# A chain of layer norms in a two-block transformer: the second norm's mean and variance from weighted moments of the first norm's centred input

## The chip, the cores and the metric

The kernel runs on one core of one Trainium2 chip. The time is the device time of one launch in microseconds (us). A core has five engines that run side by side, each through its own instruction list in order: TensorE (PE, matmuls and their weight loads), VectorE (DVE), ScalarE (ACT), GpSimd (POOL) and SyncE (SP, which here only issues DMAs). They meet through semaphores: an instruction can wait until another engine has done something, and everything queued behind it on its own engine waits too.

## What is computed

The model is a hybrid block (width 1024, 528 tokens) followed by a second block of two layers on 512 latent and 256 context tokens. All the work of this change is in the second block. Cut to the norms, one of its layers is:

```
def layer_norm(x):
    mu = jnp.mean(xf, -1, keepdims=True)
    var = jnp.mean(jnp.square(xf - mu), -1, keepdims=True)
    return (xf - mu) * lax.rsqrt(var + LN_EPS)
def modulate(x, shift, scale):
    return layer_norm(x) * (1 + scale) + shift
for l in range(2):
    h = modulate(x, sh1, sc1)                               # norm a
    y = mixing_sublayer(h, ...)
    x = layer_norm(ALPHA * x + g1 * y) * ln1_g + ln1_b      # norm b
    h = modulate(x, sh2, sc2)                               # norm c
    x = layer_norm(ALPHA * x + g2 * swiglu(h)) * ln2_g + ln2_b   # norm d
```

The output of b is the input of c, and also the residual for d. The output of d in layer 0 is the input of a in layer 1. So three times in the program a layer norm with a learned gain and bias feeds a second layer norm directly: b0 to c0, d0 to a1, b1 to c1.

## The kernel before

Everything is fp32. Activations lie transposed: the 1024 features are 8 tiles of 128 partitions, the tokens are columns, in chunks of 256: in layer 0 of the second block three chunks (the context, numbered 0, and two of latent tokens), in layer 1 two. An fp32 product is three matmuls (lines 1053 to 1055) on a high and a low half of weights and activations. SP fetches weight tiles of 128x1024, ACT makes the high half (line 1582) and DVE the low half (line 2155).

A layer norm is a chain of steps over all engines, since the sum over features is a sum over partitions, which only TensorE does cheaply:

- **mean**: eight matmuls of 128x32 ones against the eight feature tiles, four of them side by side in the four quarters of the array (`quarter_sums`, line 1235). ACT copies the four partial sums out of PSUM (`evacuate`, line 1682), and one more 128x128 matmul adds them up and spreads the result over the partitions (`total`, line 1255; step **centre**).
- DVE subtracts the mean, in two halves of 128x1024 (line 2276), and ACT squares both halves (line 1694).
- **square** and **root**: the same eight matmuls, copy and single matmul on the squares give the variance.
- ACT makes a first guess of 1/sqrt by a logarithm and an exponential (lines 1707 and 1709, `guess`), DVE corrects it with one Newton step of three 128x256 instructions (lines 2264 to 2268) after one that adds epsilon (line 2283).
- **apply**: DVE multiplies both halves by the root (line 2297), ACT applies gain and bias, one feature tile at a time (line 1730, eight instructions). A norm that feeds a matmul also needs the high and low half of its result, called X2: ACT writes the high half (line 1735), DVE the low half of the first four tiles (line 2301), POOL that of the last four (line 2855, `lows`).

ACT holds one set of function tables at a time. The logarithm and exponential need one set (loaded at line 1700), the silu of the FFN (line 1743) another, and changing is an instruction of its own on ACT.

The order of the work is planned when the program is built. `chain` (line 621) turns a list of norms and a chunk number into steps, each with the PE time it is thought to take and with the time after which the next step may follow. `woven` (line 653) runs through a list of matmul items and puts a step of a chain between two items as soon as it is due. All engines then run the same list of steps, each with its own part of a step. In a layer (`latent_sequence`, line 757) the items around a b-to-c chain are the eight output projections `oo` of each chunk; the chain of a chunk begins 2.0 after its last projection. Behind them come the FFN items `fa` and `fb`: they are taken chunk by chunk, a chunk's first only when its chain has ended, and no chunk may be more than five items ahead of the slowest. So the last chunk's chain has little to run under: once the other chunks have had their five items, TensorE waits for the last chunk's X2. The same holds at the end of layer 0, where chain d0, a1 stands before the projections of layer 1. `latent_sequence` plans chains of `[b, c_]` and of `[d, a]`, that is eight steps with two normalisations one after the other.

## Time and profile before

| | |
|---|---|
| median of 3 runs | 3517.22 us (3512.65 to 3518.37) |
| profiled execution | 3517.82 us, span of its trace 3516.0 us |
| mean granted TensorE clock | 0.967 of full speed |
| busy share | PE 93%, PEld 86%, DVE 47%, ACT 39%, POOL 13% |
| HBM | 301.57 MB read, 86 GB/s over the span |

PE is matmuls, PEld the weight loads that overlap them. Times in rows are microseconds from the start of the span. A span is the time from the first to the last instruction in the trace; the time of the execution is 1.8 us more.

The context chunk and two latent chunks of layer 0 go through b0, c0 at about 2000 to 2125, through d0, a1 at about 2640 to 2750; the two latent chunks of layer 1 go through b1, c1 at about 3045 to 3130.

### The profile page before, as it was taken

The numbers are of one execution on the slowest core, as the hardware profiler recorded it, in microseconds if no ns is written. First come the engines' busy times: TensorE is split into PE (matmuls) and PEld (weight loads), VectorE is DVE, ScalarE is ACT, GpSimd is POOL, SyncE is SP. The second block draws the span as 40 slices with busy tenths as digits, with TensorE's granted clock in tenths as the row PEclk, the third lists the DMA queues.
The fourth block names the chain that finished last, engine by engine and source line by source line (L and its number), as shares of the span: only waits on it lengthen the run. The fifth ranks groups of instructions, "written<-read, shape, count | busy, mean of one in ns | idle before, by whom it ended". The sixth has DMA issues, their size and how long they took to land. (4 is left out here: it accounts for less than half of the span.)

```text
span 3516.0 us, 59585 instructions
## 1 busy us (share of the span) xinstructions
PE 3263.2 (93%) x24536; PEld 3033.4 (86%) x24552; DVE 1661.9 (47%) x2754; ACT 1358.7 (39%) x2387; POOL 468.0 (13%) x466
## 2 busy tenths in 40 slices
PE   6999999999899899998989878999997899879998
PEld 5999987877688899997889868999995789769997
DVE  3666643447634456664346642222236436633234
ACT  3222322247623322234358553122235447542223
POOL 1010110135400010010014001000000014010100
PEclk9999999999999999999999989999998899989999
DMA  4444321111022244541102311111122202312222
GB/s 139 168 160 171 139 84 62 60 55 43 19 96 96 91 150 167 177 149 58 55 10 75 114 55 61 61 59 62 61 88 74 69 29 63 125 50 95 85 94 93
DMA packets 90379, 313.03 MB, mean 89 GB/s; under 512 B 10048, under 2 KB 14400, under 8 KB 89984
## 3 DMA queue, kind: packets, MB, share of 16 engines
q1 hardware_dynamic: 86736, 296.06, 25.2%
q0 software_dynamic: 2944, 12.63, 1.1%
q8 instruction: 198, 3.24, 0.4%
q14 instruction: 69, 0.57, 0.1%
q10 hardware_dynamic: 432, 0.52, 0.0%
HBM read 301.57 MB, written 2.10 MB: 86 GB/s over the span
## 5 line engine op out<-in xcount | busy, mean ns | idle before, releaser
L2155 DVE TENSOR_TENSOR r_Wbasel<-r_Wf,r_Wbaseh 128x1024 fp32r<-128x1024 f32 (+1 forms) x292 | 366.4, 1256 | 555.0 <-ACT r_Wbaseh L1582 554.7
L1582 ACT ACTIVATE r_Wbaseh<-r_Wf 128x1024 fp32r<-128x1024 f32 (+1 forms) x292 | 301.2, 1036 | 463.1 <-PE PS L1055 355.4
L1053 PE MATMUL PS<-r_X2h,r_Wbaseh 128*128 128x256 f32 (+1 forms) x1336 | 416.2, 311 | 51.0 <-DVE r_X2l L2301 37.3
L1053 PE MATMUL PS<-r_X1h,r_Wbaseh 128*128 128x264 f32 (+2 forms) x1216 | 393.3, 323 | 17.2 <-DVE r_Wbasel L2155 10.7
L1055 PE MATMUL PS<-r_X2h,r_Wbasel 128*128 128x256 f32 (+1 forms) x1336 | 406.1, 304 | 0.0
L1054 PE MATMUL PS<-r_X2l,r_Wbaseh 128*128 128x256 f32 (+1 forms) x1336 | 404.2, 303 | 0.0
L1054 PE MATMUL PS<-r_X1l,r_Wbaseh 128*128 128x264 f32 (+2 forms) x1216 | 380.2, 313 | 0.0
L1055 PE MATMUL PS<-r_X1h,r_Wbasel 128*128 128x264 f32 (+2 forms) x1216 | 379.6, 312 | 0.0
L2155 DVE TENSOR_TENSOR r_Wtopl<-r_Wf,r_Wtoph 128x1024 fp32r<-128x1024 f32 (+1 forms) x165 | 197.3, 1197 | 293.0 <-ACT r_Wtoph L1582 292.4
L1053 PEld LDWEIGHTS PS<-r_X2h,r_Wbaseh 128*128 128x128 f32 x1336 | 260.7, 195 | 69.2 <-ACT r_XC L1730 23.8
L1054 PEld LDWEIGHTS PS<-r_X2l,r_Wbaseh 128*128 128x128 f32 x1336 | 263.3, 197 | 11.1 <-issue 2.6
L1053 PE MATMUL PS<-r_X2h,r_Wtoph 128*128 128x256 f32 x872 | 251.2, 288 | 20.0 <-DVE r_X2l L2301 17.5
L1055 PEld LDWEIGHTS PS<-r_X2h,r_Wbasel 128*128 128x128 f32 x1336 | 260.2, 195 | 7.9
L1053 PEld LDWEIGHTS PS<-r_X1h,r_Wbaseh 128*128 128x128 f32 x1216 | 232.2, 191 | 39.6 <-DVE r_Wbasel L2155 14.2
L1054 PE MATMUL PS<-r_X2l,r_Wtoph 128*128 128x256 f32 x872 | 250.0, 287 | 0.0
L1055 PE MATMUL PS<-r_X2h,r_Wtopl 128*128 128x256 f32 x872 | 249.8, 287 | 0.0
L1054 PEld LDWEIGHTS PS<-r_X1l,r_Wbaseh 128*128 128x128 f32 x1216 | 232.5, 191 | 15.1 <-issue 2.4
L1055 PEld LDWEIGHTS PS<-r_X1h,r_Wbasel 128*128 128x128 f32 x1216 | 232.3, 191 | 13.1
L1582 ACT ACTIVATE r_Wtoph<-r_Wf 128x1024 fp32r<-128x1024 f32 (+1 forms) x165 | 168.5, 1025 | 161.0 <-PE PS L1055 86.6
L1743 ACT ACTIVATE r_TM<-PS 128x256 f32<-128x256 f32 (+1 forms) x198 | 76.3, 386 | 367.0 <-PE PS L1055 366.8
L1053 PE MATMUL PS<-r_X1h,r_Wtoph 128*128 128x264 f32 (+1 forms) x672 | 191.3, 285 | 7.8 <-DVE r_Wtopl L2155 7.8
L1054 PE MATMUL PS<-r_X1l,r_Wtoph 128*128 128x264 f32 (+1 forms) x672 | 190.9, 284 | 0.0
(369 smaller groups left out, 8727.2 us busy)
## 6 DMA issues: line engine op xcount, KB each, us to landing
r_Wf<-in_wmod SPq DMA_DIRECT2D x96, 512.0 KB, 3.5
r_Wf<-in_f_in SPq DMA_DIRECT2D x88, 512.0 KB, 4.3
r_Wf<-in_g_in SPq DMA_DIRECT2D x88, 512.0 KB, 3.4
r_Wf<-in_g_out SPq DMA_DIRECT2D x56, 448.0 KB, 3.3
r_Wf<-in_w_o SPq DMA_DIRECT2D x40, 512.0 KB, 4.4
r_Wf<-in_f_out SPq DMA_DIRECT2D x32, 448.0 KB, 4.2
r_Wf<-in_f_out SPq DMA_DIRECT2D x16, 512.0 KB, 4.4
r_Wf<-in_g_out SPq DMA_DIRECT2D x16, 512.0 KB, 3.4
```

Of the source, the lines that this page charges most:

```text
L1053: self.e.matmul(o, wh, xh, start=first, stop=False)
L1054: self.e.matmul(o, wh, xl, start=False, stop=False)
L1055: return self.e.matmul(o, wl, xh, start=False, stop=last)
L1582: e.activation(p.w(i, cols)[0], p.Wf[:, i % NW, 0:cols], ACT.Copy).then_inc(*p.hi.did(i))
L1743: e.activation(f.tm(c), p.psb(p.bank(("fa", f.tag, j, c)), f.chunks[c][1]), ACT.Silu).then_inc(*p.act.did(("silu", f.tag, j, c)))
L2155: e.tensor_tensor(l, p.Wf[:, i % NW, 0:cols], h.bitcast(F32), ALU.subtract).then_inc(*p.lo.did(i))
```

## The change

With z the centred input of the first norm, r its reciprocal root, g and b its gain and bias and b' = b - mean(b), the output is y = r g z + b. Hence

mean(y) = r mean(g z) + mean(b), and var(y) = r (r (mean(g² z²) - mean(g z)²) + 2 mean(g b' z)) + mean(b'²).

So the second norm M's statistics come from four sums over z and z² of the first norm N: z² with weights 1 and g², z with weights g and g b'. The weights are a matrix WM of 128 x 32 columns per feature tile, 16 columns each; a matrix MS picks one or the other half when the quarters are added up. `N.pair(M)` marks such a pair (b0 with c0, b1 with c1, d0 with a1). Norms d1, n1 to n3 and a0 are as before. In a pair:

- TensorE has one mean, one centre, then 16 quarter matmuls (`squares`: four each on z and z², twice) and four single matmuls (`root_sums`).
- ACT copies three partial sums instead of four, squares two halves instead of four and squares mean(g z) once (128x256).
- DVE gets five instructions of 128x256 for the second variance, and `second_applied`: it rebuilds M's centred input from y (a scalar_tensor_tensor of 128x1024), multiplies by the second root, and makes the low half. The second guess and Newton step follow without any matmul.
- Step `second` carries the second root and N's gain and bias on ACT, step `both` (once for each half) M's normalisation; ACT in `both` has half a norm: four identities and the high copy.
- POOL fetches MS (128x256) and WM (128x512 per norm) behind the attention of each layer; two steps `moments` per norm make mean(b), b', mean(b'²) and the weights (two matmuls of 8 columns and a few small DVE instructions).
- The planner has other numbers: seven steps for the pair.

```
@@ -622,6 +653,11 @@
     for N in norms:
+        if N.then is not None:
+            out += [(("mean", N, i), 1.0, 0.9), (("centre", N, i), 0.5, 4.0), (("square", N, i), 1.8, 1.5),
+                    (("root", N, i), 1.7, 7.0), (("second", N, i), 0.0, 5.0), (("both", N, i, 0), 0.0, 5.0),
+                    (("both", N, i, 1), 0.0, 7.0)]
+            continue
         if not N.rms:
...
-    chains = [(chain([b, c_], c), ("oo", l, 7, c), 2.0) for c in range(nc)]
+    chains = [(chain([b], c), ("oo", l, 7, c), 2.0) for c in range(nc)]
...
-        chains += [(chain([d, a], c), ends[c], 2.0) for c in range(nc)]
+        chains += [(chain([d], c), ends[c], 2.0) for c in range(nc)]
...
@@ -1257,6 +1305,53 @@
+    def squares(self, N, i):
...
+        for g in (0, 1):
+            e.wait_ge(*p.dve.of(("xs", N.id, i, g)))
+            x = self.quarter_sums(c, lambda k: N.xc(i, 4 * g + k), g, n, lambda k: N.weights(k, 1))
+            if g == 1:
+                x.then_inc(*p.mm.did(("cross", N.id, i)))
+            e.wait_ge(*p.act.of(("sq", N.id, i, g)))
+            x = self.quarter_sums(b, lambda k: N.sq4(i, g)[:, k, :], g, n, lambda k: N.weights(k, 0))
+        x.then_inc(*p.mm.did(("square", N.id, i)))
+
+    def root_sums(self, N, i):
...
+        e.matmul(p.psb(b, n), one, ss, start=True, stop=True).then_inc(*p.mm.did(("var", N.id, i)))
...
+        e.matmul(p.psb2(b, 0, n), one, sc, start=True, stop=True)
+        e.matmul(p.psb2(b, 256, 256 + n), two, ss, start=True, stop=True).then_inc(
+            *p.mm.did(("gz", N.id, i), ("squares", N.id, i)))
...
+        e.matmul(p.psb(b, n), two, sc, start=True, stop=True).then_inc(
+            *p.mm.did(("gbz", N.id, i), ("crosses", N.id, i)))
@@ -1623,6 +1718,15 @@
...
+        elif what == "square" and a[0].then is not None:
+            N, i = a
+            self.evacuate(N, "crosses", "cross", i, 1.0 / 1024)
+            self.evacuate(N, "squares", "square", i, 1.0 / 1024)
+        elif what == "second":
+            self.second_root(*a)
+            self.first_applied(*a)
+        elif what == "both":
+            self.second_applied(*a)
@@ -1715,6 +1822,36 @@
...
+    def second_root(self, N, i):
+
+        self.e.wait_ge(*self.p.dve.of(("var2", N.id, i)))
+        self.guess_of(N.row(i, 3), N.row(i, 2), N.bvar, ("guess2", N.id, i))
+
+    def first_applied(self, N, i):
+        p, e = self.p, self.e
+        for g in (0, 1):
+            e.wait_ge(*p.dve.of(("xn", N.id, i, g)))
...
+    def second_applied(self, N, i, g):
...
+        e.wait_ge(*p.dve.of(("xn", M.id, i, g)))
...
+        e.wait_ge(*p.act.of(("end", M.id, i, 4 * g + 3)))
+        e.activation(M.to4(i, g, 0), M.xc4(i, g), ACT.Copy).then_inc(*p.act.did(("high", M.id, i, g)))
@@ -2284,6 +2430,80 @@
...
+    def first_root(self, N, i):
...
+        self.newton(x, r, t, p.act.of(("guess", N.id, i)), 1.0, ("rsqrt", N.id, i))
...
+        e.tensor_tensor(u, ggzz, u, ALU.subtract).then_inc(*dve.did(k("gvar")))
+        e.wait_ge(*dve.of(k("gvar")))
+        e.tensor_tensor(u, u, r, ALU.mult).then_inc(*dve.did(k("gvar_r")))
+        e.wait_ge(*p.mm.of(k("gbz")))
+        e.wait_ge(*dve.of(k("gvar_r")))
+        e.scalar_tensor_tensor(u, p.psb(p.bank(k("gbz")), n), 2.0, u, ALU.mult, ALU.add).then_inc(
+            *dve.did(k("twice")))
+        e.wait_ge(*dve.of(k("twice")))
+        e.tensor_tensor(v, u, r, ALU.mult).then_inc(*dve.did(k("var2")))
+        e.tensor_tensor(gzr, gz, r, ALU.mult).then_inc(*dve.did(k("gzr")))
+        self.scaled_by_root(N, i, 0, r)
...
+    def second_root(self, N, i):
...
+        e.tensor_scalar(x, v, N.bvar, None, ALU.add).then_inc(*dve.did(("eps2", N.id, i)))
+        self.scaled_by_root(N, i, 1, r)
+        e.wait_ge(*dve.of(("eps2", N.id, i)))
+        self.newton(x, y, t, p.act.of(("guess2", N.id, i)), 1.0, ("rsqrt2", N.id, i))
+
+    def second_applied(self, N, i, g):
...
+        e.wait_ge(*p.act.of(("end", N.id, i, 4 * g + 3)))
+        e.scalar_tensor_tensor(M.xc4(i, g), N.h4(i, g), N.bmean, N.wide(N.row(i, 1), i), ALU.subtract,
+                               ALU.subtract).then_inc(*dve.did(("xs", M.id, i, g)))
+        e.wait_ge(*dve.of(("xs", M.id, i, g)))
+        e.tensor_tensor(M.xc4(i, g), M.xc4(i, g), N.wide(N.row(i, 3), i), ALU.mult).then_inc(
+            *dve.did(("xn", M.id, i, g)))
```

How the lists move, first on TensorE, in layer 1, where the last chunk's b stands together with chunk 0's second norm. Names are the program's: r_H holds b's input and, in place, its centred and normalised form, r_SQ the squares, r_PA the partial sums, r_CF the ones, r_WM and r_MS the new weights, r_X2h and r_X2l the input of the FFN. Before:

```order
L1235 MATMUL PS<-r_H,r_CF 32x256 x16
L1255 MATMUL PS<-r_PA,r_CF 128x256 x2
L1235 MATMUL PS<-r_SQ_114,r_CF 32x256 x16
L1255 MATMUL PS<-r_PA,r_CF 128x256 x2
L1053 MATMUL PS<-r_X2h,r_Wtoph 128x256
L1054 MATMUL PS<-r_X2l,r_Wtoph 128x256
```

After:

```order
L1284 MATMUL PS<-r_H,r_CF 32x256 x8
L1303 MATMUL PS<-r_PA,r_CF 128x256
L1284 MATMUL PS<-r_H,r_WM 32x256 x4
L1284 MATMUL PS<-r_SQ_114,r_WM 32x256 x4
L1284 MATMUL PS<-r_H,r_WM 32x256 x4
L1284 MATMUL PS<-r_SQ_114,r_WM 32x256 x4
L1346 MATMUL PS<-r_PA,r_MS 128x256
L1349 MATMUL PS<-r_PA,r_MS 128x256
L1350 MATMUL PS<-r_PA,r_MS 128x256
L1353 MATMUL PS<-r_PA,r_MS 128x256
L1093 MATMUL PS<-r_X2h,r_Wtoph 128x256
L1094 MATMUL PS<-r_X2l,r_Wtoph 128x256
```

Chunk 0's second mean and variance, which shared the place with the last chunk's first ones, are gone. Further on, before, the last chunk's own second mean and variance stood among the FFN matmuls (eight of line 1235 and one of line 1255, each twice); after, none does.

On ACT, same place, from the high halves of weights through the end of chunk 0's b. Here r_Wtoph and r_Wbaseh are high halves of weights, r_H is b's result (line 1730, 1840 after), r_XC_121 is c's (1851 after). Before:

```order
L1707 ACTIVATE r_RS<-PS,r_V 128x256
L1709 ACTIVATE r_RS<-r_RS 128x256
L1730 ACTIVATE r_H<-r_H,r_V 128x256 x8
L1582 ACTIVATE r_Wtoph<-r_Wf 128x1024
L1582 ACTIVATE r_Wbaseh<-r_Wf 128x1024 x2
L1682 ACTIVATE r_PA<-PS 128x256 x2
L1694 ACTIVATE r_SQ_114<-r_XC_121 128x4x256 x2
L1694 ACTIVATE r_SQ_114<-r_H 128x4x256 x2
```

After:

```order
L1677 ACTIVATE r_Wtoph<-r_Wf 128x1024
L1677 ACTIVATE r_Wbaseh<-r_Wf 128x1024 x2
L1814 ACTIVATE r_SQ_114<-r_SQ_114,r_MB 128x256
L1816 ACTIVATE r_SQ_114<-r_SQ_114 128x256
L1840 ACTIVATE r_H<-r_H,r_V 128x256 x8
L1786 ACTIVATE r_PA<-PS 128x256
L1798 ACTIVATE r_SQ_114<-r_H 128x4x256 x2
L1851 ACTIVATE r_XC_121<-r_XC_121,r_MOD 128x256 x4
```

The three copies of weights moved ahead of the eight instructions that apply b's gain, and the second guess (1814, 1816) stands ahead of those eight. The last chunk's partial sum (1786) now comes behind them. On DVE the new small instructions stand between the first root and the first wide multiplication, and weight splits and residual additions between the two wide ones:

```order
L2468 TENSOR_TENSOR r_SQ_114<-PS,r_SQ_114 128x256
L2470 TENSOR_TENSOR r_SQ_114<-r_SQ_114,r_RS 128x256
L2473 SCALAR_TENSOR_TENSOR r_SQ_114<-PS,r_SQ_114 128x256
L2476 TENSOR_TENSOR r_SQ_114<-r_SQ_114,r_RS 128x256
L2477 TENSOR_TENSOR r_SQ_114<-PS,r_RS 128x256
L2482 TENSOR_TENSOR r_H<-r_H,r_RS 128x4x256
L2292 TENSOR_TENSOR r_Wtopl<-r_Wf,r_Wtoph 128x1024
L2553 SCALAR_TENSOR_TENSOR r_H<-PS,r_MOD,r_H 128x256
L2292 TENSOR_TENSOR r_Wbasel<-r_Wf,r_Wbaseh 128x1024
```

What was one piece of two multiplications (line 2297 before) is now two, with other work between them: three weight splits (2292) and three residual additions (2553) in all.

## Rows read from the trace of the kernel before

**Rows 1.** The page, busy time, share of the span and instructions of each engine
```profile
PE 3263.2 (93%) x24536; PEld 3033.4 (86%) x24552; DVE 1661.9 (47%) x2754; ACT 1358.7 (39%) x2387; POOL 468.0 (13%) x466
```

**Rows 2.** Waits of TensorE: line, releaser, us in total, times, longest
```profile
PE PS L1053 <- DVE r_X2l L2301: 54.8, 7, 9.6
```

**Rows 3.** Stretches: length, busy us (and count) of PE PEld DVE ACT POOL, PEclk, DMA
```profile
2150.00:2600.00 450.00, 450.00 (x3753) 450.00 (x3752) 108.62 (x157) 95.10 (x164) 39.91 (x54) 1.00 0.19 61
2057.85:2123.49 65.64, 41.65 (x305) 35.98 (x305) 24.35 (x31) 39.09 (x61) 7.63 (x6) 0.81 0.08 28
2695.61:2748.22 52.61, 29.16 (x160) 20.09 (x161) 22.96 (x26) 28.78 (x48) 4.71 (x2) 0.63 0.03 10
3068.88:3126.91 58.03, 33.63 (x209) 25.24 (x209) 26.20 (x30) 34.58 (x55) 6.18 (x4) 0.68 0.08 29
```

**Rows 4.** Timeline, b1 and c1 of the last chunk: start, us, engine, instruction, [idle before]
```profile
3039.38 1.07 PE L1235 MATMUL PS<-r_H,r_CF 128*32 128x256 f32 x16
...
3068.88 0.38 ACT L1682 ACTIVATE r_PA<-PS 128x256 f32<-128x256 f32 x1 [3.83 <-PE PS L1235]
3070.02 2.35 DVE L2276 TENSOR_TENSOR r_XC<-r_H,PS 128x1024 f32<-128x1024 f32 x2 [2.42 <-PE PS L1255]
...
3092.66 4.04 ACT L1730 ACTIVATE r_H<-r_H,r_V 128x256 f32<-128x256 f32 x8 [4.12 <-DVE r_H L2297]
3097.67 1.28 ACT L1743 ACT_TABLE_LOAD   x1
3099.24 0.38 ACT L1682 ACTIVATE r_PA<-PS 128x256 f32<-128x256 f32 x1
3102.32 0.59 PE L1255 MATMUL PS<-r_PA,r_CF 128*128 128x256 f32 x2
3102.95 2.35 DVE L2276 TENSOR_TENSOR r_XC<-r_H,PS 128x1024 f32<-128x1024 f32 x2
...
3113.19 1.28 ACT L1700 ACT_TABLE_LOAD   x1
3114.48 0.47 ACT L1707 ACTIVATE r_RS<-PS,r_V 128x256 f32<-128x256 f32 x1
3116.88 2.36 DVE L2297 TENSOR_TENSOR r_XC<-r_XC,r_RS 128x1024 f32<-128x1024 f32 x2
3118.20 2.08 ACT L1730 ACTIVATE r_XC<-r_XC,r_MOD 128x256 f32<-128x256 f32 x4 [2.80 <-DVE r_XC L2297]
3120.31 1.06 ACT L1735 ACTIVATE r_X2h<-r_XC 128x1024 fp32r<-128x1024 f32 x1
3121.40 1.22 DVE L2301 TENSOR_TENSOR r_X2l<-r_XC,r_X2h 128x1024 fp32r<-128x1024 f32 x1 [2.16 <-ACT r_X2h L1735]
3122.77 0.55 PE L1053 MATMUL PS<-r_X2h,r_Wtoph 128*128 128x256 f32 x1 [9.61 <-DVE r_X2l L2301]
3124.50 2.35 POOL L2855 TENSOR_TENSOR r_X2l<-r_XC,r_X2h 128x1024 fp32r<-128x1024 f32 x1 [14.05 <-ACT r_X2h L1735]
3126.91 0.58 PE L1053 MATMUL PS<-r_X2h,r_Wtoph 128*128 128x256 f32 x1 [1.24 <-POOL r_X2l L2855]
```

**Rows 5.** Groups by line and shape, 2625 to 3130: count, busy us, mean ns, idle before
```profile
L1694 ACT ACTIVATE r_SQ<-r_H 128x1024 f32<-128x1024 f32 x10 | 10.6, 1060 | 9.7 <-DVE r_H L2276 9.2
L1682 ACT ACTIVATE r_PA<-PS 128x256 f32<-128x256 f32 x20 | 7.6, 378 | 25.3 <-PE PS L1235 25.2
L2268 DVE SCALAR_TENSOR_TENSOR r_RS<-r_RS 128x256 f32<-128x256 f32 x11 | 4.7, 425 | 0.4
```

**Rows 6.** Groups by line and shape, the whole trace
```profile
L2241 DVE SCALAR_TENSOR_TENSOR r_JK<-r_Wf,r_CR 128x1024 f32<-128x1024 f32 x96 | 117.0, 1218 | 0.0
L1235 PE MATMUL PS<-r_SQ,r_CF 128*32 128x256 f32 x368 | 30.3, 439 | 7.9 <-ACT r_SQ L1694 4.2 <-DVE r_XC L2276 3.3
```

More of the change, by code:

```diff
@@ L667, in woven @@
             out.append(s)
-            if s[0] == "root":
+            if s[0] == "root" and s[1].then is None:
                 out.append(("apply", *s[1:]))
@@ L1167, in step @@
         elif what == "square":
-            self.square(*a)
+            if a[0].then is None:
+                self.square(*a)
+            else:
+                self.squares(*a)
         elif what == "root":
-            self.root_sum(*a)
+            if a[0].then is None:
+                self.root_sum(*a)
+            else:
+                self.root_sums(*a)
+        elif what == "moments":
+            self.moments(*a)
         elif what == "mod":
@@ L2195, in step @@
         elif what == "root":
-            self.root_norm(*a)
+            if a[0].then is None:
+                self.root_norm(*a)
+            else:
+                self.first_root(*a)
+        elif what == "second":
+            self.second_root(*a)
+        elif what == "both":
+            self.second_applied(*a)
+        elif what == "moments":
+            self.moments(*a)
         elif what == "apply":
@@ L2286, in root_norm, with moments @@
         self.newton(x, y, t, p.act.of(("guess", N.id, i)), 1.0, ("rsqrt", N.id, i))
+    def moments(self, N, last):
+        p, e, dve = self.p, self.e, self.p.dve
+        key = ("bvar" if last else "bmean", N.id)
+        e.wait_ge(*p.mm.of(key))
+        e.tensor_reduce(N.bvar if last else N.bmean, p.psb(p.bank(key), 8), AX, ALU.add).then_inc(*dve.did(key))
+        e.wait_ge(*dve.of(key))
+        if not last:
+            e.tensor_scalar(N.b1, p.vec8(N), N.bmean, None, ALU.subtract).then_inc(*dve.did(("b1", N.id)))
+            e.wait_ge(*dve.of(("b1", N.id)))
+            e.tensor_tensor(N.b2, N.b1, N.b1, ALU.mult).then_inc(*dve.did(("bsquare", N.id)))
+            return
+        e.tensor_scalar(N.bvar, N.bvar, N.then.eps, None, ALU.add).then_inc(*dve.did(("bvar2", N.id)))
+        e.wait_ge(*p.load(("moments", N.id)).of("in"))
+        w = N.WM[:, :, 16:32]
+        e.tensor_tensor(w, w, w, ALU.mult).then_inc(*dve.did(("gg", N.id)))
+        w = N.WM[:, :, 48:64]
+        e.tensor_tensor(w, w, N.b1.unsqueeze(2).broadcast_to([128, 8, 16]), ALU.mult).then_inc(
+            *dve.did(("weights", N.id)))
@@ L2827, in step @@
             self.lows(*a)
+        elif what == "both":
+            N, i, g = a
+            if g == 1:
+                self.lows(N.then, i)
         elif what == "bar":
@@ L3241, in _layout @@
     a["vec"] = v
+    g = np.stack([cols(i[f"ln{n}_g_2"][l]) for n, l in ((1, 0), (2, 0), (1, 1))])
+    g = np.broadcast_to(g[:, :, :, None, None], (3, 128, 8, 2, 32)).copy()
+    g[:, :, :, 0, 0:16] = 1.0
+    a["wmom"] = g
     return a
```

120 lines of the change are left out of this document (110 added, 10 removed).

## The prediction

> **What bounds the kernel now.** I read the page's busy times first. TensorE is busy 3263.2 of 3516.0 us, 93% [rows 1], so a gain must come out of the 253 us in which it idles, or out of stretches where it runs at a lowered clock. Then the waits of TensorE: the largest group by far is the first matmul on X2, 54.8 us in seven waits, the longest 9.6 [rows 2]. X2 is what the second norm of a pair hands to the FFN or to the next projections. Then the stretches: from 2150 to 2600, in the middle of an FFN, TensorE is busy 450.00 of 450.00 us at full clock, while DVE and ACT have 109 and 95. In the three stretches from the last chunk's first mean to the second half of its X2 it is busy 41.65 of 65.64, 29.16 of 52.61 and 33.63 of 58.03 us, at a granted clock of 0.81, 0.63 and 0.68 of full [rows 3], between its two levels. They hold 24.0, 23.5 and 24.4 us of idle time, 72 in all, and no other engine is full either. The bound there is the chain of small steps of the last chunk. Since TensorE is full behind each of them, what is saved there reaches the end of the program.
>
> The timeline shows that chain for b1, c1 of the last chunk [rows 4]. The mean's partial sums are copied at 3068.88; b is done at 3096.70 (3092.66 + 4.04); c then needs a table load and silu of the FFN that stand before its copy on ACT, its copy at 3099.24, its single sum at 3102.32, centring at 3102.95, squares and their sums, a table load at 3113.19, the guess at 3114.48, multiplication 3116.88, gain 3118.20, high half 3120.31, low half 3121.40, TensorE at 3122.77; the second half waits for POOL until 3126.91. From b's end to c's guess there are 17.8 us (3114.48 - 3096.70). This is the piece that the change rewrites.
>
> **The change part by part.** *Removed from the path, per pair:* c's mean, copy, sum, centring, two squares, eight sums, copy and sum, that is those 17.8 us.
>
> *Put in its place.* After N's root DVE has five more small instructions: 425 ns each [rows 5]. Between the logarithm's end (3114.48 + 0.47) and the multiplication at 3116.88 [rows 4] lie four of this kind in a chain, so one costs 0.46 to 0.48 with its hop, and five 2.3 us. ACT squares mean(g z), 0.4 us by the 378 of a copy of the same shape [rows 5]. The second guess then only needs the second variance, and runs on ACT ahead of N's gain; its Newton step lies beside the eight gain instructions (4.04 us [rows 4]). Behind these DVE rebuilds M's centred input with a wide scalar_tensor_tensor: 1218 ns for 128x1024 in another place of the program [rows 6], the same as the subtraction (2.35 for two [rows 4]), and multiplies it, 1.2. So from N's gain to M's gain stand 2.4 us on DVE in place of about 18 to 20.
>
> *TensorE's own work.* Sixteen quarter matmuls took 1.07 us at full clock [rows 4], 439 ns each as single records, which overlap [rows 6]. Before a pair had 32 quarter matmuls and four single ones, now it has 24 (8 + 16) and five (1 + 4): at 1.07 per 16 and 0.3 each that is 2.14 + 1.2 = 3.3 before, 1.6 + 1.5 = 3.1 after. Nothing of note; at half clock twice that.
>
> *ACT* loses two squares of 1.06 and one copy of 0.38 [rows 5] and gains 0.42; *DVE* has 2.3 us more in small and as many wide instructions as before (nine). Over eight pairs ACT has 17 us less, DVE 18 more, at 47% busy; only what of it is on the chain counts.
>
> *The moments and the new DMAs.* POOL fetches MS and WM when the attention is done, ahead of all output projections (no row shows such a load); POOL is at 13% [rows 1], TensorE gets two matmuls of 8 columns per norm. I cost them at nothing, covered by the output projections; if the cover fails, each of three places waits a few us for a load, 10 us at most in all, which is inside the range.
>
> *The order.* On ACT the last chunk's first copy now stands behind the eight gain instructions of chunk 0, and these wait for DVE's second wide multiplication, which stands behind three weight splits and three residual additions. So it comes later: 3069.7 by my walk, against 3068.88. I walked every engine's list of the changed program through this stretch, giving each instruction the later of its operands and its engine, with the durations of these rows:
> - copy of the mean 3069.7 (+0.8); centring 3070.9 to 3073.25; meanwhile DVE rebuilds M of chunk 0 until 3075.65, and ACT has its gain and high half until 3078.9, then copies the two partial sums of the last chunk (3079.7).
> - four single sums at half clock, 3082.9; ACT, busy with the second half of chunk 0, comes to the first guess at 3083.3 to 3083.8 and the small square at 3084.3.
> - Newton 3085.3, five small ones 3087.6, first wide multiplication 3088.8; then ACT has a weight split, a gated FFN tile with its high half and a table load before the second guess, 3094.5.
> - gain of N 3098.5 (eight, 4.04); another table load and a silu, 3100.2; M's rebuild and multiplication 3103.1 behind a gating on DVE; four gains and high half 3106.3; low half, TensorE 3107.7 (before 3122.77 [rows 4]); the second half through POOL 3112.3 (before 3126.91).
>
> That is 14.6 us. Of the 17.8 removed and 2.4 put in, 15.4 would be left if nothing else moved; 2.3 for small instructions and 1 for the late start count against it, and the new order gives some of it back. The same walk gives, for layer 0's b0, c0, X2 of the last chunk at 2105.1 in its second half against the end of the first stretch, 2123.49 [rows 3]: 18.4. For d0, a1 it gives 2731.7 against 2748.22 [rows 3]: 16.5. The sum is 49.5. The stretches have 24.0, 24.4 and 23.5 us of idle time, so no term asks for more than there is, and the same matmuls (33.63 us of 43.4 left for b1) still fit. The walk has ideal hops between engines in some places, 0.1 to 0.2 us each; I take 1.5 off for them: 48.
>
> Sum against the profiled execution: 3517.8 - 48 = 3469.8. It stands 0.6 above the median, which is less than I can tell: 3470.
>
> *A rule that speaks against.* The trace has a table load of 1.28 us at 3113.19 and the guess at 3114.48 [rows 4], 0.01 after its end, so no drain is seen behind a load. The path of the last chunk has two table loads more than before in b0, c0 and one more in b1, c1, since guess and silu now alternate; that is in the walk. The Trainium skill, "ScalarE: Activation LUTs", section "What ACT_TABLE_LOAD costs", gives 1283 ns for the load and about 1380 ns for a drain with each. By that page three more loads would cost an estimated 4 us more and the time be about 3474; the row shows the load alone, and I go by it.
>
> **Bounds of what the trace does not show.** The quarter matmuls with different weights in the four quarters: the nearest rows are 1.07 for sixteen with equal weights, and 439 ns each if they did not lie side by side. At the upper end, 16 x 0.44 = 7.0 in place of 1.07 x (1 to 2), some 5 more per pair and up to 40 for eight pairs if none of it is hidden. I take the lower end, since the weight loads are instructions of the same kind. Wide scalar_tensor_tensor with a row broadcast over four tiles and a per-partition scalar: 1.22 for the subtraction with the same broadcast, 1.22 for the row of this operation; a second operand in SBUF instead of PSUM may do either way, at most 0.3 each, 2 us in all. The new loads 0 to 10. The walk's placing of FFN items in ACT's and DVE's lists: each misplaced item delays a step by 1 to 1.7 (a split of 128x1024 as the square 1.06 [rows 5], table load and a copy-sized silu 1.28 + 0.38 [rows 4, 5]); two or three per place give minus 12 to plus 10 in all.
>
> **Rivals.**
> - *Half the gain.* ACT takes its list in order, and between root and second guess stand splits, gatings, silus that wait for TensorE, which itself waits. If at each place another round of these (table load, silu, load back, about 4, twice) falls on the path, the gain is 8 less each: 24 in all, 3494. For: TensorE's wait for the last X2 was 9.6 us with one such round on the path [rows 2, 4]. Against: the walk already has each of these items.
> - *Quarter sums not side by side.* 40 less of 49.5: gain 10, 3508. For: weights now differ for each quarter and each tile, so each needs its own load. Against: before, every quarter matmul has its own load record too, and they ran at 1.07 per 16.
> - *The waits only move.* The last chunk's X2 stays where it was, because something else (weights, partial sums of the FFN in order) ends there: 3517. Against: the seven waits name DVE's X2l [rows 2], and nothing else ends there.
> - *Slower.* One mechanism: the late first guess. The second root and N's gain are now one step and stand behind FFN items; if the chunk ahead of the last also comes later, TensorE runs out earlier, its clock falls, and the sums at half clock (3.1 x 2) and copies are all on the path. Price: copy 3.3 later (three copies of weights), sums 2.4 more, per place 5.7 with nothing saved by the shorter second chain: 17 over three places, 3535. It decides if the last chunk's X2 begins more than 54 us after its first copy (3122.77 - 3068.88 = 53.9 [rows 4]).
>
> **How the numbers follow.** A measurement of this kernel tells apart about 0.2%, 7 us. Forecast 0.68, its own range 3457 to 3484 (the placing and the loads). Half the gain 0.17 at 3494. Sums not side by side 0.03 at 3508. Waits only move 0.05 at 3517. Slower 0.07 at 3535. The range 3450 to 3503 holds the first two, about 0.85 less the edges. Faster by more than 7 us: 0.68 + 0.17 + 0.03 = 0.88; same 0.05; slower 0.07.
>
> **What the profile after would show.** The wait of TensorE for r_X2l falls from 54.8 to below 30 us. In the three places from the last chunk's first copy to its second half of X2: about 43 us for b1 (58.0 before), 46 for b0 (65.6), 36 for d0 (52.6). Sixteen quarter sums with WM in about 1.1 us at full clock. The last chunk's second guess about 11 us after its first. Busy times: ACT down 17, DVE up about 18, PE the same. I am wrong if the stretches shorten and the time does not, if X2's first half still begins 50 us or more after the copy, or if the copy itself comes over 3 us later than TensorE's last output projection would have it.

## The result

The changed kernel takes 3465.95 us (median of 4 runs, 3461.35 to 3469.64), the kernel before on the same occasion 3517.80. The ratio is 0.9854, 95% interval 0.9837 to 0.9871: a gain of 51.9 us, 1.5%. The forecast was 3470 with its own range 3457 to 3484. Later, beside the experiments, the same kernel gave 0.9862 (0.9849 to 0.9876), 3469.8 us.

The span of the profiled execution is 3459.5 us, 56.5 less than before. Its busy times, page part 1:

```profile
PE 3237.1 (94%) x24436; PEld 3021.6 (87%) x24452; DVE 1679.3 (49%) x2815; ACT 1338.9 (39%) x2369; POOL 479.2 (14%) x471
```

Against [rows 1] ACT has 19.8 us less and DVE 17.4 more, close to the 17 and 18 of the forecast. TensorE has 26 us less at 100 records less, where the forecast had "the same". An estimated 9 us of it are the fewer and shorter sums (below); for the rest I can only argue that less of its work falls in stretches of lowered clock, since the mean granted clock rose from 0.967 to 0.972.

The waits of TensorE (line, releaser, us, times, longest):

```profile
PE PS L1093 <- DVE r_X2l L2505: 26.4, 3, 10.3
PE PS L1303 <- ACT r_PA L1786: 14.0, 8, 4.7
PE PS L1316 <- DVE r_MB L2444: 7.8, 1, 7.8
PE PS L1093 <- DVE r_X2l L2521: 5.5, 1, 5.5
```

The first row and the last together answer to [rows 2], since a norm outside the pairs now makes its low half at a line of its own: 31.9 us in four waits where there were 54.8 in seven. That is a little above the forecast's "below 30". Six of the seven lay at the three places, two at each, 49.3 us; now there is one at each, for the last chunk, 26.4 us. The second row is TensorE waiting for the copy of a mean's partial sums. The third is new: it is a moment step of d0, planned between two output projections. TensorE stood 7.8 us in it, because the instruction it waits for is behind the first root of another chunk on DVE.

The three stretches that answer to those of [rows 3], from the last chunk's first copy of partial sums to the second half of its X2, and the same part of b1's timeline as in [rows 4]:

```profile
2054.80:2102.40 47.60, 33.26 (x254) 30.77 (x253) 25.47 (x32) 30.83 (x53) 9.40 (x6) 0.86 0.07 23
2672.68:2708.07 35.39, 20.23 (x127) 15.69 (x127) 23.50 (x27) 22.84 (x42) 4.74 (x2) 0.76 0.00 1
3026.80:3070.37 43.57, 26.23 (x174) 21.71 (x174) 26.86 (x31) 28.85 (x49) 7.46 (x4) 0.71 0.08 26
```

```profile
3026.80 0.36 ACT L1786 ACTIVATE r_PA<-PS 128x256 f32<-128x256 f32 x1
...
3039.84 0.46 ACT L1814 ACTIVATE r_RS<-PS,r_V 128x256 f32<-128x256 f32 x1
...
3041.99 1.28 ACT L1880 ACT_TABLE_LOAD   x1
...
3049.62 0.42 ACT L1890 ACTIVATE r_H3h<-r_TM 128x256 fp32r<-128x256 f32 x1 [4.08 <-DVE r_TM L2529]
...
3050.05 1.28 ACT L1804 ACT_TABLE_LOAD   x1
...
3051.35 0.51 ACT L1814 ACTIVATE r_SQ<-r_SQ,r_MB 128x256 f32<-128x256 f32 x1
...
3056.26 1.28 ACT L1880 ACT_TABLE_LOAD   x1
3057.56 0.38 ACT L1880 ACTIVATE r_TM<-PS 128x256 f32<-128x256 f32 x1
3058.03 0.42 DVE L2529 TENSOR_TENSOR r_TM<-r_TM,PS 128x256 f32<-128x256 f32 x1 [4.28 <-ACT r_TM L1880]
3058.37 1.28 DVE L2498 SCALAR_TENSOR_TENSOR r_XC<-r_H,r_MB,r_SQ 128x1024 f32<-128x1024 f32 x1
...
3061.41 2.08 ACT L1851 ACTIVATE r_XC<-r_XC,r_MOD 128x256 f32<-128x256 f32 x4 [2.50 <-DVE r_XC L2501]
...
3065.97 0.55 PE L1093 MATMUL PS<-r_X2h,r_Wtoph 128*128 128x256 f32 x1 [10.30 <-DVE r_X2l L2505]
...
3070.37 0.58 PE L1093 MATMUL PS<-r_X2h,r_Wtoph 128*128 128x256 f32 x1 [1.50 <-POOL r_X2l L3088]
```

After the pair's four single sums, the last of which ends at 3040.75, no sum over features stands on the chain any more. The second guess is 11.5 us later (forecast about 11). X2's first half comes 39.2 us after the first copy; before it was 53.9. The stretches are 47.6, 35.4 and 43.6 us; the forecast said 46, 36 and 43.

Single profiles differ by several us outside the three places: the changed kernel's profile and its repeat are 3.4 us apart at the start of b0 and 8.7 at the end of b1, while the places themselves agree to 0.4 us. So from here on I compare the three *places* by their length: each from a copy of chunk 0's partial sums (in b0 that of its squares, in a pair the first of the two copies; in d0 and b1 that of its mean) to TensorE's first matmul on the second half of the last chunk's X2. Each number is the difference of two starts in a timeline.

| kernel | b0 | d0 | b1 | sum | ratio to before (95%) | median us |
|---|---|---|---|---|---|---|
| before | 124.66 | 119.16 | 86.40 | 330.2 | | 3517.8 |
| changed | 107.66 | 100.68 | 71.95 | 280.3 | 0.9854 (0.9837 to 0.9871) | 3465.95 |
| changed, repeat | 107.69 | 100.68 | 72.27 | 280.6 | 0.9862 (0.9849 to 0.9876) | 3469.8 |
| b, c pairs only | 107.11 | 119.15 | 71.78 | 298.0 | 0.9910 (0.9894 to 0.9927) | 3482.6 |
| d, a pair only | 127.49 | 100.68 | 86.80 | 315.0 | 0.9952 (0.9937 to 0.9967) | 3497.8 |
| before, earlier steps | 124.01 | 122.71 | 87.02 | 333.7 | 1.0002 (0.9993 to 1.0012) | 3517.6 |
| ten more on DVE | 119.91 | 113.53 | 81.35 | 314.8 | 0.9950 (0.9935 to 0.9964) | 3497.5 |
| moments early | 107.13 | 100.67 | 71.86 | 279.7 | 0.9844 (0.9829 to 0.9859) | 3459.75 |
| second at 1.0 | 109.50 | 106.49 | 75.80 | 291.8 | 0.9900 (0.9884 to 0.9917) | 3480.95 |
| second and both at 1.0 | 111.68 | 105.08 | 70.3 | 287.1 | 0.9889 (0.9874 to 0.9904) | 3476.8 |
| split gain | 103.12 | 97.34 | 68.16 | 268.6 | 0.9833 (0.9817 to 0.9848) | 3458.2 |
| combined | 102.02 | 97.37 | 68.16 | 267.6 | 0.9823 (0.9809 to 0.9836) | 3454.3 |
| combined, lows on POOL | 105.74 | 98.8 | 68.47 | 273.0 | 0.9833 (0.9819 to 0.9847) | 3460.8 |
| combined, no silu | 101.02 | 96.17 | 65.35 | 262.5 | 0.9793 (0.9779 to 0.9806) | 3444.35 |

The three places give 17.0 + 18.5 + 14.5 = 49.9 us of the gain, measured from the unrounded sums. The stretch from 3126.91 to the end of the span before and from 3070.37 after is 389.1 us in both.

### The profile page after: what moved, and what is told of

The parts are those of the page before. It is cut to its first block and busy times, and to the rows that moved or that the text cites. A ratio compares the mean times of both kernels' runs of the same rounds, so it can differ in the third digit from the quotient of the medians.

```text
span 3459.5 us, 59413 instructions
## 1 busy us (share of the span) xinstructions
PE 3237.1 (94%) x24436; PEld 3021.6 (87%) x24452; DVE 1679.3 (49%) x2815; ACT 1338.9 (39%) x2369; POOL 479.2 (14%) x471
## 5 line engine op out<-in xcount | busy, mean ns | idle before, releaser
L1093 PE MATMUL PS<-r_X1h,r_Wbaseh 128*128 128x264 f32 (+2 forms) x1216 | 391.2, 322 | 17.6 <-DVE r_Wbasel L2292 11.4
L1093 PE MATMUL PS<-r_X2h,r_Wtoph 128*128 128x256 f32 x872 | 249.4, 286 | 11.8 <-DVE r_X2l L2505 10.3
L3045 POOL TENSOR_TENSOR r_H3l<-r_TM,r_H3h 128x256 fp32r<-128x256 f32 x110 | 84.5, 768 | 793.1 <-ACT r_H3h L1890 793.1
```

Source lines behind the costliest of these rows:

```text
L1093: self.e.matmul(o, wh, xh, start=first, stop=False)
L3045: e.tensor_tensor(hl, f.tm(c), hh.bitcast(F32), ALU.subtract).then_inc(*p.pool.did(("hid", f.tag, j, c)))
```

## The experiments

### One kind of pair alone

Edit for b, c only:

```
-        self.norms["d0"].pair(self.norms["a1"])
...
-        items[-2:-2] = [(("moments", d, False), 0, None)]
-        items.append((("moments", d, True), 0, None))
...
-        chains += [(chain([d], c), ends[c], 2.0) for c in range(nc)]
+        chains += [(chain([d, p.norms["a1"]], c), ends[c], 2.0) for c in range(nc)]
...
```

> Only b0 to c0 and b1 to c1 are pairs; d0 and a1 are as in the kernel before. My theory: the gain is made at three separate places, each by the last chunk's shorter chain, and adds up. The trace of the changed kernel puts 21.1 us at b0, 19.1 at d0 and 16.4 at b1. So this run has a span 37.5 us shorter than before (about 3478.5) and TensorE's place between d0 and a1 looks as before, 52.6 us. Rival: the gain is a matter of the new step numbers and orders over the whole layer, and the places are not independent; then this run is more than 6 us away from that.

Measured: 3482.6 us, ratio 0.9910; span 3474.9. The place at d0 is 119.15 us, before 119.16; b0 and b1 are those of the changed kernel within 0.6. The pairs' gains are independent: what the sum claimed. (The span is 41.1 us shorter than before, not 37.5, which is still within the 6 us; the places give 17.55 + 14.62 = 32.2, the rest of the span's difference lies outside them, 6.5 of it ahead of b0.)

For d, a only the edit is the mirror image (`b.pair(n)` and its moment steps out, `chain([b, c_], c)` back in, MS waited for in d0).

> Only d0 to a1 is a pair. By my theory (independent places) the span is 19 us shorter than before, about 3497; if the places are not independent it is more than 6 us away. A third possibility: without the other pair the two small moment steps of d0, which held TensorE 7.8 us in the changed kernel, cost another amount, since their neighbours change; then their wait shows it.

Measured: 3497.8 us, ratio 0.9952, span 3497.5. The place at d0 is 100.68 us, the same hundredth as in the changed kernel. b0 is 127.49, 2.8 us *longer* than before, though b0 and c0 work as before: the moment steps of d0 stand in it. TensorE waits there:

```profile
2052.73 0.57 PE L1313 MATMUL PS<-r_MB,r_CF 128*128 128x8 f32 x2 [13.10 <-DVE r_MB L2441]
```

Thirteen us of waiting stand beside 2.8 us in the place. In the kernel before TensorE also waited in this part of b0, at other instructions: 9.6 us in four waits, the longest 4.6. So there are only 3.5 us more of waiting, and that is near what the place lost. That the steps are the cause is read from the row; no run has this kernel with them elsewhere. The medians add up as the places do: 34.8 us for b, c alone and 19.7 for d, a alone, 54.5 together, against 51.9 for both.

### The order alone

```
-        out += [(("square", N, i), 1.0, 0.9), (("root", N, i), 0.5, 8.5 if N.dst is None else 7.5 if N.rms else 9.0)]
+        out += [(("square", N, i), 1.0, 0.9), (("root", N, i), 0.5, 5.0 if N.dst is None else 7.5 if N.rms else 9.0)]
```

> The kernel before, with one number of the planner changed: the norms b and d finish their apply step 5.0 instead of 8.5 after the root, as near as the steps of the changed kernel stand. If the gain is the arithmetic (a second mean and variance taken off the chain), this gives at most 3 us per place and at most 9 in all, more likely 0 to 4. If the gain is mostly the new order of steps among FFN items, it gives 20 us or more.

Measured: ratio 1.0002 (0.9993 to 1.0012), d0 even 3.5 us longer. Earlier steps without the new arithmetic give nothing. So the gain is what was taken off the chain, as far as one number of the planner can show it: the changed kernel's order differs in more than this number, and that order as a whole was not tried without the new arithmetic.

### Ten more small instructions

```
+        for j in range(10):
+            e.tensor_tensor(gzr, gz, r, ALU.mult).then_inc(*dve.did(k(f"again{j}")))
+            e.wait_ge(*dve.of(k(f"again{j}")))
         e.tensor_tensor(gzr, gz, r, ALU.mult).then_inc(*dve.did(k("gzr")))
```

> The changed kernel with ten more 128x256 instructions on DVE per pair, behind the second variance and ahead of the first wide multiplication (the same product made again). They take about 10 x 0.46 = 4.6 us. By my theory the last chunk's chain sets the end at all three places, so the span grows by 10 to 14 us, 4.6 at each less what stands hidden behind ACT's wait for the FFN items ahead of the second guess. Rival: at these places the chain waits for in-order FFN items (table loads, gatings) and not for DVE's arithmetic; then it grows by 5 or less.

Measured: 3497.5 us, 34.5 us more at the three places, and 35.1 in the span. Both theories fall, mine by a factor of about two and a half even at its upper end. The ten take 4.54 us:

```profile
3078.11 4.54 DVE L2478 TENSOR_TENSOR r_SQ<-PS,r_RS 128x256 f32<-128x256 f32 x10
```

The stretches of this kernel, first those from the copy of chunk 0 to the last chunk's first copy, then those from there on:

```profile
1995.46:2064.60 69.14, 52.04 (x421) 47.66 (x414) 54.44 (x90) 36.28 (x59) 2.41 (x1) 0.90 0.31 106
2620.88:2695.32 74.44, 55.43 (x455) 49.48 (x455) 56.22 (x88) 38.38 (x63) 2.41 (x1) 0.90 0.29 96
3026.26:3059.15 32.89, 26.09 (x226) 23.31 (x226) 25.14 (x41) 16.10 (x25) 0.00 (x0) 0.94 0.35 116
2064.60:2115.37 50.77, 33.67 (x259) 31.18 (x257) 29.62 (x42) 30.82 (x53) 9.39 (x6) 0.85 0.07 22
2695.32:2734.41 39.09, 20.81 (x127) 16.40 (x127) 27.65 (x37) 22.94 (x42) 4.72 (x2) 0.63 0.00 0
3059.15:3107.61 48.46, 26.00 (x174) 21.47 (x175) 31.09 (x41) 28.84 (x49) 7.45 (x4) 0.76 0.07 25
```

In the changed kernel the first three are these:

```profile
1994.74:2054.80 60.06, 51.59 (x424) 47.96 (x417) 46.05 (x70) 36.18 (x59) 2.40 (x1) 0.91 0.36 121
2607.39:2672.68 65.29, 55.31 (x455) 49.61 (x455) 47.74 (x68) 38.42 (x63) 2.41 (x1) 0.92 0.35 109
2998.42:3026.80 28.38, 25.66 (x226) 23.27 (x226) 20.96 (x31) 16.01 (x25) 0.00 (x0) 1.00 0.42 137
```

So the last chunk's own stretch grows by 3.2, 3.7 and 4.9, 11.8 in all, as my theory had it. But the part ahead of it grows by 9.1, 9.2 and 4.5: two earlier chunks in b0 and d0, one in b1, 4.5 to 4.6 us for each, every bit of the ten instructions. DVE works its list in order, and behind a chunk's small instructions stand the weight splits and residual additions of the next projections, on which the last chunk's mean depends. Per instruction it is 34.5 / 80 = 0.43 us. The change itself added five to each of eight pairs: if the rate holds for them too, which no run tests, they take back an estimated 17 us. I had costed them at 2.3 us per place, 7 in all, with only part of the rest in the walk.

### The moment steps earlier

```
+        if l == 0 and m in (3, 6):
+            items.append(("moments", d, m == 6))
...
-        items[-2:-2] = [(("moments", d, False), 0, None)]
-        items.append((("moments", d, True), 0, None))
+        pass
```

> The changed kernel with d0's two moment steps planned among chunk 0's output projections, behind b0's, in place of the end of the projections, where TensorE waited 7.8 us in them. My theory: that wait is in front of FFN work that is done ahead anyway, and counts only as far as it makes the last chunk's first mean late. The run with b, c pairs alone, which has no such step, was 3.6 us better at these places than the changed kernel's share (41.1 against 37.5). So the span falls by 3 to 4 us, to about 3456. If the wait is fully on the path it falls by 7 to 8, if it is hidden by less than 1.

Measured: the wait is gone, and the places are 0.6 us shorter, 0.5 of them in b0. In the combined kernel the same edit gives 1.1 in b0 (102.02 against 103.12 with the split alone). The median of 3459.75 lies 6.2 us below the changed kernel's, the span of the profile 3.1 above it; the intervals of the two ratios overlap, so the times say nothing more. My 3 to 4 came from a difference of spans (41.1 - 37.5) that was mostly offset outside the places. The places say under 1, as the third case had it. The trace shows why so little comes of it. With the moment steps gone, TensorE waits a few us later for the same DVE list, for the residual additions ahead of the last chunk's mean, and then for that mean's copy:

```profile
2054.02 1.08 PE L1285 MATMUL PS<-r_H,r_CF 128*32 128x256 f32 x8 [6.44 <-DVE r_H L2554]
2060.45 0.67 PE L1304 MATMUL PS<-r_PA,r_CF 128*128 128x256 f32 x2 [1.42 <-ACT r_PA L1787]
```

In the changed kernel neither of the two waited over 0.6 us. So the wait of 7.8 us did not end, it moved: DVE sets the time at which the last chunk can start, and TensorE idles for it at one instruction or at another.

### The second guess ahead of FFN items

```
-                    (("root", N, i), 1.7, 7.0), (("second", N, i), 0.0, 5.0), (("both", N, i, 0), 0.0, 5.0),
-                    (("both", N, i, 1), 0.0, 7.0)]
+                    (("root", N, i), 1.7, 1.0), (("second", N, i), 0.0, 5.0), (("both", N, i, 0), 0.0, 5.0),
+                    (("both", N, i, 1), 0.0, 13.0)]
```

> The changed kernel with the step second planned 1.0 instead of 7.0 behind the root, and the last step's number raised by the same 6, so that TensorE's own order is nearly the same, while on ACT and DVE the second guess stands ahead of some FFN items. The last chunk's second variance was ready at 3045.5 and its guess ran at 3051.35, behind a silu, a gated high half and a table load. If these in-order items hold the chain, the three places gain 3 to 6 us each and the span falls by 9 to 18. The rival is that ACT and DVE then wait in the step while TensorE needs weight splits queued behind it, for five pairs that are not the last chunk's: then it gains nothing or loses up to 10.

Measured: 3480.95 us, the places 11.5 us longer. The last chunk's own stretches are 43.3, 32.3 and 40.6 us, that is 4.3, 3.1 and 2.9 *shorter*: what stood in front of the second guess did hold the chain. The last chunk's second guess now comes 4.3 us after its first at all three places, in the changed kernel 9.3, 7.7 and 11.5. But the parts ahead of them grow more:

```profile
1999.91:2066.07 66.16, 55.12 (x430) 50.54 (x422) 48.43 (x72) 39.55 (x63) 2.35 (x1) 0.92 0.33 110
2612.81:2686.96 74.15, 56.69 (x455) 50.41 (x455) 50.40 (x70) 41.76 (x68) 2.35 (x1) 0.90 0.30 96
3013.77:3048.94 35.17, 26.09 (x226) 23.31 (x226) 23.41 (x33) 19.26 (x31) 0.00 (x0) 0.92 0.33 110
```

by 6.1, 8.9 and 6.8. Both theories are right, each in its part of the place; the rival is larger, and with 11.5 us at the places, 15.0 in the medians, larger than the 10 it was given. An edit of this kind for the last chunk alone was not tried.

> As the run before it, but the two steps both also planned at 1.0 each (the last number raised again). The whole second half of the pair then stands on ACT and DVE in one piece, with almost no FFN item inside. By the theory that in-order items hold the last chunk's chain this gains 2 to 3 us more per place for the table load and silu between N's gain and M's (3056.26 to 3057.94 in the changed kernel); by the rival (weight splits late for TensorE) it is slower than the run before it, by up to 15.

Its edit is 1.0 also for `second` and the first `both`, 21.0 for the last. Measured: 3476.8 us, places 287.1, 6.8 above the changed kernel and 4.7 below the run before it. In b1 it is 1.6 us better than the changed kernel, in b0 and d0 4.0 and 4.4 worse. Against the run before it b1 gains 5.5 and d0 1.4, and b0 loses 2.2, so neither the theory's 2 to 3 us per place nor the rival's loss came; the intervals of the two ratios overlap.

### The gain instructions split

```
             self.second_root(*a)
-            self.first_applied(*a)
+            self.first_applied(*a, 0)
         elif what == "both":
+            if a[2] == 0:
+                self.first_applied(*a[:2], 1)
             self.second_applied(*a)
...
```

> The changed kernel with the second four of N's eight gain instructions moved on ACT from the step second into the first step both, ahead of M's first four. M's first half needs only the first four, so DVE's rebuild and multiplication (2.5 us) then lie beside the second four (2.1 us), and the next chunk's first copy no longer waits for DVE's second wide multiplication. Expected 2 us less at each of the three places and about 1 for the earlier copy in b1, so the span falls by 5 to 8. If the gatings of the FFN hold DVE at that point anyway, it falls by less than 2.

Measured: 3458.2 us, ratio 0.9833; the places are 4.5, 3.3 and 3.8 us shorter, 11.7 in all, more than the 5 to 8 I said; the medians differ by 7.7, within them, with intervals of the ratios that overlap. Of these only 2.3, -0.4 and 1.2 lie in the last chunk's own stretch, 3.1 together. The larger part is ahead: the last chunk's first copy comes 2.2, 3.8 and 2.6 us sooner after chunk 0's. In b1 of the changed kernel it stood behind chunk 0's second four gain instructions, which waited 3.71 us for DVE:

```profile
3023.57 1.22 DVE L2482 TENSOR_TENSOR r_H<-r_H,r_RS 128x1024 f32<-128x1024 f32 x1
...
3024.82 2.07 ACT L1840 ACTIVATE r_H<-r_H,r_V 128x256 f32<-128x256 f32 x4 [3.71 <-DVE r_H L2482]
...
3026.80 0.36 ACT L1786 ACTIVATE r_PA<-PS 128x256 f32<-128x256 f32 x1
```

In the split kernel it waits for nothing but the matmuls:

```profile
3012.55 2.07 ACT L1842 ACTIVATE r_H<-r_H,r_V 128x256 f32<-128x256 f32 x4
...
3017.74 0.39 ACT L1788 ACTIVATE r_PA<-PS 128x256 f32<-128x256 f32 x1 [3.13 <-PE PS L1284]
```

### Both together, and two variants of it

The changed kernel was run again beside them.

> The changed kernel once more, beside the three that follow, for a comparison on one chip. Expected as before: 51 to 53 us less than the kernel before, ratio 0.985. The stretches from the first copy of partial sums of chunk 0 to the last chunk's second half of X2 repeat within 1 us, though the spans of single profiles differ by several us upstream of them.

> The split gain instructions and the early moment steps together. The split alone shortened the three places by 4.5, 3.3 and 3.8 us (11.7 in all, 7.7 in the medians), the early moments by 0.5. So 8 to 12 us less than the changed kernel, ratio to the kernel before about 0.982. If the split's gain was one lucky profile, it is under 4.

Measured: 3454.3 us against 3469.8 for the changed kernel on the same chip, ratios to before 0.9823 and 0.9862 with intervals that don't meet (0.9809 to 0.9836, 0.9849 to 0.9876). The places are 12.7 us shorter than the changed kernel's and the median 15.5, both above the 8 to 12 expected. This version beats both kernels, 1.8% below the kernel before. The repeat's places agree with the first profile to 0.4 us, as expected; its gain is 45.3 us by the medians, 44 to 53 by the ratio's interval, where 51 to 53 was expected.

For the next, on top of the combined kernel:

```
...
-        if g == 1:
-            e.wait_ge(*p.act.of(("high", M.id, i, 0)))
-            e.tensor_tensor(M.to4(i, 0, 1), M.xc4(i, 0), M.to4(i, 0, 0).bitcast(F32), ALU.subtract).then_inc(
-                *dve.did(("low", M.id, i, 0)))
...
-            if g == 1:
-                self.lows(N.then, i)
+            self.lows(N.then, i, g)
...
```

> As the combined one, and in a pair the first low half of X2 is made by POOL (2.35 us) in place of DVE (1.22), so DVE has 8 x 1.22 = 9.8 us less in the pairs. Ten more small instructions of 4.6 us per pair cost 34.5 of 36.8 us at the three places, so nearly all of DVE's work in a pair counts, that of the earlier chunks too. If that holds for this instruction, 5 to 9 us less than the combined one. Rival: what counts is DVE's work ahead of the second root alone; the low half comes last, where the last chunk's DVE is idle, and POOL is 1.13 us slower at it and slows DVE when both run (a 0.42 us instruction took 1.82 beside it): then the same or up to 5 slower.

Measured: 3460.8 us, places 5.5 us longer than the combined kernel's (3.7, 1.4 and 0.3). The rival is right, at the edge of its "up to 5"; the medians differ by 6.5, the intervals of the ratios overlap. What DVE is spared here comes last in a pair, and POOL's longer instruction stands in front of TensorE:

```profile
3065.35 2.35 POOL L3086 TENSOR_TENSOR r_X2l<-r_XC,r_X2h 128x1024 fp32r<-128x1024 f32 x1 [4.42 <-ACT r_X2h L1857]
...
3067.84 0.55 PE L1094 MATMUL PS<-r_X2h,r_Wtoph 128*128 128x256 f32 x1 [9.51 <-POOL r_X2l L3086]
```

So "nearly all of DVE's work in a pair counts" was too wide: shown is only that of the place where the ten stood.

For the last, also on top of it:

```
-        self.logs = False
-        e.activation(f.tm(c), p.psb(p.bank(("fa", f.tag, j, c)), f.chunks[c][1]), ACT.Silu).then_inc(
+        e.activation(f.tm(c), p.psb(p.bank(("fa", f.tag, j, c)), f.chunks[c][1]), ACT.Copy).then_inc(
```

> As the combined one, but the silu of the FFNs is left out (a plain copy of the same tile takes its place), so that ACT never changes tables in the FFNs. It measures what the changes of tables cost on the chain. By the rows a load is 1.28 us with nothing behind it; 4 of them lie between the last chunk's first copy and its X2 in b0 and 3 in b1, some beside waits. That gives 4 to 9 us less than the combined one. With 1.38 us more per change for a drain, as the Trainium skill has it (ScalarE: Activation LUTs, What ACT_TABLE_LOAD costs), it would be 9 to 18. Less than 3 if they all lie beside waits.

Measured: 3444.35 us, 9.9 below the combined kernel; span 11.4 less, but only 5.0 of it at the places (1.0, 1.2 and 2.8), the rest outside them, 5.5 ahead of b0, where FFNs stand too and where profiles of one kernel differ by as much. The kernel has 12 loads fewer, nine of them in the places (five, one and three). So 9.9 us is just outside my 4 to 9, and the times alone do not part the two sums, since 9.9 lies in 9 to 18 as well. The 5.0 at the places speak for the first: nine loads of 1.28 are 11.5 us, of which some lie beside waits, and the one load of d0 is worth 1.2. What decides is that the rows leave no time for a drain (below). A kernel whose silu needs no other table would be faster by some of this; that is a bound and not a proposal.

## Why the prediction was right

**The bound and the places.** Right. Three places, independent of each other, and all that was saved there reached the end: 389.1 us remain behind the last one in both kernels.

**The sum.** 49.5 by the walk, 49.9 in the places. By place it was 18.4, 16.5 and 14.6; measured 17.0, 18.5 and 14.5. The two off by 1.4 and 2.0 cancel, and that they do is luck. The 1.5 taken off for hops, which made 48 of 49.5, was not needed. The median fell by 51.9. For b0 the last chunk's first copy came 1.0 us later in the place than before (60.06 against 2057.85 - 1998.83 = 59.02), for d0 1.3 sooner (65.29 against 66.55), in b1 the same (28.38 against 28.37). The 0.8 of the walk for b1 did not come; the forecast of its stretch, 42.6 by the walk and 43 in the text, was 43.57.

**TensorE's own work.** A wrong reading that did no harm. I took the x16 of [rows 4] for sixteen matmuls. It is eight: the order of the changed program shows x8 for a mean where the trace has x16, so each of these matmuls leaves two records (those of lines 1053 to 1055 leave one). The real numbers are 32 quarter matmuls before at 8 per 1.07 us, 4.3 us per pair, and 24 after. The changed kernel's sixteen with different weights:

```profile
3007.53 0.64 PE L1284 MATMUL PS<-r_H,r_WM 128*32 128x256 f32 x8
3007.98 0.61 PE L1284 MATMUL PS<-r_SQ,r_WM 128*32 128x256 f32 x8
3008.41 0.61 PE L1284 MATMUL PS<-r_H,r_WM 128*32 128x256 f32 x8
3008.85 0.61 PE L1284 MATMUL PS<-r_SQ,r_WM 128*32 128x256 f32 x8
```

These are four groups of four at a pitch of 0.43 to 0.45 us, 1.9 us in all, against 0.5 per four before. So different weights in the four quarters run side by side just as well, and the rival of sums that don't is refuted. My "1.6 after" was 3.0 (1.07 + 1.9), "2.14 before" 4.3, and "about 1.1" for the sixteen with WM 1.9: the term is a gain of 1.3 us per pair at full clock. The single sums took 0.6 us each where I had 0.3, 2.4 for four before; after, one alone and four in a row from 3012.36 to 3014.25 make 2.5. That leaves a gain of 1.2 us per pair where I had 0.2, an estimated 9 us of TensorE's time in eight pairs, though TensorE has slack there.

**The small instructions on DVE.** Right for the last chunk, too small for the others. This is the largest term that I mis-sized: at 0.43 us for each of 40 it is an estimated 17 us, against the 7 that the text names. Why the sum came out nonetheless is argued and not shown: the walk went through the lists of the chunk ahead too and so held part of the rest, and d0 gained 2.0 more than the walk gave.

**The moments.** Costed at nothing with the output projections as cover. The cover failed in b0: a wait of 7.8 us, worth 0.5 to 1.1 in the places, since TensorE otherwise waits for the same DVE list a little later; 13.1 us and 2.8 where b and c are not a pair. The loads of MS and WM made nobody wait.

**Wide scalar_tensor_tensor.** 1.28 us where [rows 6] gave 1.22 and I allowed up to 0.3 more.

**Table loads.** 3050.05 + 1.28 = 3051.33, and the guess starts at 3051.35, as before in [rows 4]; ACT's instruction before the load ended at 3050.04 (3049.62 + 0.42). So there is no drain behind a load and none ahead of it, and the sum by the row was the right one. By the drain of the Trainium skill ("ScalarE: Activation LUTs", "What ACT_TABLE_LOAD costs") the run without silu should have gained 9 us or more at the places, an estimate; it gained 5.0. One premise was wrong: b0's last chunk has not two loads more on ACT between its first copy and its X2, but one fewer, four where there were five. In b1 it is three where there were two, as said, and the whole program has 32 where it had 34.

**The rivals.** "Half the gain" did not come; the walk had each in-order item already, as I had argued. "Waits only move" and "slower" did not come; but two of their parts are real. In-order items do hold the last chunk's chain (its stretches were 3 to 4 us shorter with the second guess ahead of them), and the late first copy costs 2.2 to 3.8 us per place, which the split removed. Against the kernel before the copy was at most 1.0 us later; that the pair's missing sums of the earlier chunks paid for the rest was not tested.

## What to carry to other kernels

Where a chain of small steps sets the end, take whole steps off it, by algebra if need be; then price what was added on every engine's list for *all* chunks, since in-order lists can make the earlier chunks' small instructions as dear as the last one's (the ten ahead of the first multiplication were; the low half, last in a pair, was not). A long instruction group that waits for another engine should be cut where the next consumer needs only its first half: one such cut gave a further 12 us at the places here, 8 in the medians. A wait that is taken away may only move to the next instruction that needs the same list, as the 7.8 us of the moment steps did. And compare stretches between marks within the profile, not spans: here two profiles of one kernel were 8 us apart in their spans and 0.4 in the places.

## What the runs showed of the hardware

A DVE instruction of 128x256 that reads two SBUF operands took 1.84 us in place of 0.42 when a POOL instruction was under way as it started; one that read PSUM half a us before it, beside the same POOL instruction, took its normal 0.42:

```profile
3040.02 2.39 POOL L3088 TENSOR_TENSOR r_X2l<-r_XC,r_X2h 128x1024 fp32r<-128x1024 f32 x1 [78.21 <-ACT r_X2h L1854]
...
3040.33 0.42 DVE L2462 TENSOR_SCALAR r_RS<-PS 128x256 f32<-128x256 f32 x1 [2.73 <-ACT r_RS L1814]
...
3040.85 1.84 DVE L2410 TENSOR_TENSOR r_RS<-r_RS 128x256 f32<-128x256 f32 x1
```

POOL's ended at 3042.41 and DVE's 0.28 later. It goes the other way too. The low half of a hidden tile took POOL 0.74 us alone and 1.25 beside wide DVE instructions, one of which took 1.63 in place of 1.22:

```profile
3058.98 1.25 POOL L3045 TENSOR_TENSOR r_H3l<-r_TM,r_H3h 128x256 fp32r<-128x256 f32 x1 [7.39 <-ACT r_H3h L1890]
3059.68 1.63 DVE L2501 TENSOR_TENSOR r_XC<-r_XC,r_SQ 128x1024 f32<-128x1024 f32 x1
...
3089.72 0.74 POOL L3045 TENSOR_TENSOR r_H3l<-r_TM,r_H3h 128x256 fp32r<-128x256 f32 x1 [5.01 <-ACT r_H3h L1890]
```

The Trainium skill, "SBUF — State Buffer", section "SBUF: two separate sides", says that GpSimd and a VectorE instruction with two SBUF inputs share one pair of ports, which is held for a whole instruction while the other blocks. The rows agree: 1.84 us is the 1.56 until POOL's end and 0.28 more. In b1 of both kernels this puts 1.4 us on the last chunk's chain, in the first root's Newton step.
